# Feed-forward of the spatial block: seven products of halves for 20 of 22 column pairs, the down projection as its own phase

## What is computed

```python
def _conv_ffn(x, w_up, conv_f_w, conv_f_b, w_down):      # w_up 1024 x 5632, w_down 2816 x 1024
    h = _causal_depthwise_conv(x @ w_up, conv_f_w, conv_f_b)   # 3 taps along the 1024 rows
    gate, val = h[..., :D_FF_2], h[..., D_FF_2:]
    return (jax.nn.silu(gate) * val) @ w_down

x = _layernorm(DEEPNORM_ALPHA * x + ffn, ln2_g, ln2_b)
```

## Time and profile before

| | |
|---|---|
| median of 3 runs | 3779.22 us (3771.41 to 3779.77) |
| profiled execution: span, first to last instruction | 3767.9 us |
| its own time | not given apart from the runs; span and what lies around it, some 11 us at the median |
| PE busy | 3631.0 us, 96% |
| DVE, ACT, POOL busy | 57%, 34%, 48% |
| granted TensorE clock, mean | 0.987 |
| the stage `ffn`, first up matmul to the end of the span | from 3012.9 us |

### The profile page before, as it was taken

The page is one execution under the profiler, slowest core; times in us unless marked ns, Lnnn a source line. Parts: engine busy times, 40 slices in busy tenths (PEclk is TensorE's granted clock), DMA queues, the critical chain, the costliest instruction groups (busy, mean ns, idle before and its releaser), DMA issues.

```text
span 3767.9 us, 51125 instructions
## 1 busy us (share of the span) xinstructions
PE 3631.0 (96%) x17973; PEld 2944.0 (78%) x17973; DVE 2148.5 (57%) x3586; ACT 1263.4 (34%) x2051; POOL 1812.5 (48%) x1926
## 2 busy tenths in 40 slices
...
DMA packets 244572, 223.53 MB, mean 59 GB/s; under 512 B 12586, under 2 KB 194488, under 8 KB 244425
## 3 DMA queue, kind: packets, MB, share of 16 engines
...
## 4 chain that ended last, share of the span: by engine, by line
PE 59%; DVE 4%; ACT 2%; POOL 1%; issue 1%; DVEq 0%; ACTq 0%; POOLq 0%
PE PS L749 6%; PE PS L750 6%; PE PS L751 6%; PE PS L1219 3%; PE PS L1220 3%; PE PS L1221 3%; PE PS L776 3%; PE PS L778 3%; PE PS L777 3%; PE PS L871 2%; PE PS L869 2%; PE PS L870 2%; PE PS L883 2%; PE PS L885 2%; PE PS L884 2%; PE PS L1265 2%
## 5 line engine op out<-in xcount | busy, mean ns | idle before, releaser
L749 PE MATMUL PS<-UH,WH 128*128 128x512 f32 x1808 | 716.8, 396 | 22.4 <-ACT UU L2213 8.0
L3748 POOL TENSOR_SCALAR WH<-RAW 128x1024 fp32r<-128x1024 f32 x203 | 226.0, 1113 | 1033.0 <-issue 386.4
L3751 POOL TENSOR_TENSOR WL<-RAW,WH 128x256 fp32r<-128x256 f32 x809 | 704.1, 900 | 16.9
L751 PE MATMUL PS<-UH,WL 128*128 128x512 f32 x1808 | 708.1, 392 | 0.0
L750 PE MATMUL PS<-UL,WH 128*128 128x512 f32 x1808 | 707.9, 392 | 0.0
L749 PEld LDWEIGHTS PS<-UH,WH 128*128 128x128 f32 x1808 | 340.8, 188 | 103.1 <-issue 15.7
L751 PEld LDWEIGHTS PS<-UH,WL 128*128 128x128 f32 x1808 | 340.3, 188 | 73.8
L750 PEld LDWEIGHTS PS<-UL,WH 128*128 128x128 f32 x1808 | 341.0, 189 | 70.2 <-issue 0.2
L2423 DVE TENSOR_TENSOR X<-PS,X 128x512 f32<-128x512 f32 x320 | 215.3, 686 | 222.7 <-PE PS L935 213.5
L3376 DVE SCALAR_TENSOR_TENSOR FY<-FZ,PV,FY 128x512 f32<-128x512 f32 x88 | 82.9, 942 | 329.8 <-ACT FY L2343 328.9
L933 PE MATMUL PS<-WH,HH 128*128 128x512 f32 x640 | 253.9, 397 | 10.3 <-POOL WL L3751 5.6
...
## 6 DMA issues: line engine op xcount, KB each, us to landing
RAW<-in_mlp_w_dram SPq DMA_DIRECT2D x104, 512.0 KB, 4.2
...
RAW<-in_w_up_dram SPq DMA_DIRECT2D x44, 512.0 KB, 3.9
ADR<-in_ada_w_dram ACTq DMA_DIRECT2D x32, 512.0 KB, 3.8
WR<-in_od_w_in_dram SPq DMA_DIRECT2D x32, 512.0 KB, 4.2
W2R<-in_mlp_w_dram SPq DMA_DIRECT2D x24, 512.0 KB, 3.3
RAW<-in_w_down_dram SPq DMA_DIRECT2D x22, 512.0 KB, 3.2
RAW<-in_ev_w_in_dram SPq DMA_DIRECT2D x20, 512.0 KB, 3.8
```

Source lines behind the costliest of these rows:

```text
L749: pe.matmul(bank(b)[0:width], wh, xh, start=(k == 0), stop=False)
L751: mm = pe.matmul(bank(b)[0:width], wl, xh, start=False, stop=(k == NK - 1))
L3748: pool.tensor_scalar(WH[slot][:, 0:n], r[:, 0:n], 1.0, 1.0, ALU.mult, ALU.mult).then_inc(S("w_hi"), 1)
L3751: ins = pool.tensor_tensor(WL[slot][:, c], r[:, c], WH[slot][:, c].bitcast(F32), ALU.subtract)
```

## The change

The first two column pairs go as before (`up`). For each of the other 20, a round: x's transpose is cut in quarters (features 0 to 511 or 512 to 1023, tokens 0 to 511 or 512 to 1023), the pair's weights too (gate or val, upper or lower 512 features), and the four quarters of the result come from seven products, p1 to p7, in place of eight. US1, US2, US3 and UH's fourth quarter hold sums of quarters of x, made once by ACT, DVE and POOL. FT1, FT2, and the differences of p7 and p4 are made anew in each round by DVE (`t1_t2`, `t4`) and POOL (`t3`), and each of seven weight operands is split by ACT (`w_hi`) and POOL (`w_lo`) into one buffer per name. Products add up in banks b = r % 2, 6 and 7; ACT (`copy`) and DVE (`sum_`) take intermediate sums from a bank into GZ before the next product is added to it. ACT's `tap_2` writes the last tap into PSUM banks 2 to 5, DVE's `conv` adds the two others there, `silu` and `gated` make the result in FO, and SP writes it to DRAM (`ffn_gated`).

Then 11 blocks of the down projection: SP reads two row blocks back (FRAW, 1 MB), ACT and DVE split them (`f_hi`, `f_lo`), POOL splits w_down, PE does 16 items of 6 matmuls a block. The residual is scaled on DVE in rounds 2 to 9 (`residual`), from row vectors loaded by DMA; POOL's `resid(5, ...)` and PE's `t_rows(5, ...)` are gone. Semaphores are reused (`past` gives one with the count it starts from). The core of the diff, with its indentation shortened:

```diff
+FF_PLAIN = 2
+FF_ROUNDS = D_FF2 // P - FF_PLAIN
+FF_DOWN = D_FF2 // P // 2
+FF_SLOT = {"p1": (0, 0), "p2": (0, 1), "p6": (1, 0), "p5": (3, 0), "p7": (2, 0), "p3": (2, 1), "p4": (3, 1)}
+FF_ORDER = ("p1", "p2", "p6", "p5", "p7", "p3", "p4")
+FF_NTH = {name: i + 1 for i, name in enumerate(FF_ORDER)}
+FF_RES = 16
...
-    def down_half(h, order):
-        h_ready.take(2)
...
+    def product(r, name, b, start):
+        pe.wait_ge(*past("fp_lo", 7 * r + FF_NTH[name]))
+        xh, xl, k0, c = moving[name]
+        wh, wl = FPH[name], FPL[name]
+        for k in range(4):
+            if r == 0 and name in made:
+                pe.wait_ge(*past(made[name], k + 1))
+            w = slice(k * P, (k + 1) * P)
+            pe.matmul(bank(b), wh[:, w], xh[:, k0 + k, c], start=start and k == 0, stop=False, skip_group_check=True)
+            pe.matmul(bank(b), wh[:, w], xl[:, k0 + k, c], start=False, stop=False, skip_group_check=True)
+            mm = pe.matmul(bank(b), wl[:, w], xh[:, k0 + k, c], start=False, stop=(k == 3), skip_group_check=True)
+        mm.then_inc(S("fp_mm"), 1)
...
+    def round_(r):
+        b = r % 2
+        if r >= 2:
+            pe.wait_ge(*past("fp_c", 4 * (r - 1)))
+        product(r, "p1", b, True)
+        if r:
+            pe.wait_ge(*past("fp_d", 3 * (r - 1) + 1))
+        product(r, "p2", 6, True)
+        pe.wait_ge(*past("fp_c", 4 * r + 1))
+        product(r, "p6", b, False)
+        if r:
+            pe.wait_ge(*past("fp_d", 3 * r))
+        product(r, "p5", 7, True)
+        pe.wait_ge(*past("fp_c", 4 * r + 2))
+        product(r, "p7", b, False)
+        pe.wait_ge(*past("fp_c", 4 * r + 3))
+        product(r, "p3", 7, False)
+        pe.wait_ge(*past("fp_d", 3 * r + 2))
+        product(r, "p4", b, False)
...
+    def down(j, h, order):
+        s = j % 2
...
+            n = 16 * j + 8 * h + i
+            if n < 8:
+                name, count = FD_ENTRY[n]
+                pe.wait_ge(*past(name, count))
+            else:
+                pe.wait_ge(*past("fd_add", n - 7))
...
+            pe.wait_ge(*past("fd_w", 2 * j + 2 if h or order != BY_COLUMN[0] else 2 * j + mh + 1))
+            for k in range(2):
+                if i == 0:
+                    pe.wait_ge(*past("fd_lo", 4 * j + 2 * h + k + 1))
...
     up(0, 0, fresh)
-    t_rows(5, 0, 1)
     up(0, 1)
-    t_rows(5, 2, 3)
     t_u(5, 1, 0, 1)
     up(0, 2, None, {2: (2,), 5: (3,)})
     up(0, 3, None, {2: (4,), 5: (5,)})
     t_u(5, 1, 6, 7)
-    d_free.wait_at(ND)
-    with rounds(pe, ph["count"] - 1, (w_ready, 6), (a_free, 8), (d_free, 16), (h_ready, 4)) as it:
-        for m in range(4):
-            up(1, m, fresh if m == 0 else None)
-        down_half(0, BY_COLUMN[0])
-        for m in range(4):
-            up(0, m)
-        down_half(1, BY_COLUMN[1])
     for m in range(4):
-        up(1, m)
-    down_half(0, BY_BLOCK[0])
-    down_half(1, BY_BLOCK[1])
+        up(1, m, fresh if m == 0 else None)
+    a_free.wait_at(NA)
+    for r in range(FF_ROUNDS):
+        round_(r)
+    for j in range(FF_DOWN):
+        last = j == FF_DOWN - 1
+        for h in range(2):
+            down(j, h, (BY_BLOCK if last else BY_COLUMN)[h])
...
+    def w_hi(r, name):
+        if r == 0:
+            act.wait_ge(S("gemm_done"), item0 + 5 + FF_SLOT[name][0])
+        else:
+            act.wait_ge(*past("fp_mm", 7 * (r - 1) + FF_NTH[name]))
+        sem, count = {"p1": ("f_ra", 16 * (r + 1)), "p2": ("f_ra", 16 * (r + 1)), "p3": ("f_rb", 16 * (r + 1)),
+                      "p6": ("ft2", r + 1), "p5": ("ft1", r + 1), "p7": ("ft3", r + 1), "p4": ("ft4", r + 1)}[name]
+        act.wait_ge(*past(sem, count))
+        act.activation(FPH[name][:, :], src[name], ACT.Copy).then_inc(S("fp_hi"), 1)
+    def copy(r, nth, out, b):
+        act.wait_ge(*past("fp_mm", 7 * r + nth))
+        act.activation(out, bank(b), ACT.Copy).then_inc(S("fp_c"), 1)
...
+    def tap_2(r, m, z, b):
+        c = r + FF_PLAIN + 22 * m
+        act.activation(bank(b), z, ACT.Identity, bias=taps("conv_f_b_2", c), scale=taps("conv_f_w_2", c, 2))\
+            .then_inc(S("fp_y"), 1)
+    z = [GZ[:, m, 2 + h * HALF:2 + (h + 1) * HALF] for m in range(2) for h in range(2)]
+    def last_gate(r):
+        copy(r, 7, z[1], r % 2)
+        act.wait_ge(*past("fp_c", 4 * r + 4))
+        if r:
+            act.wait_ge(*past("fp_s", 2 * r))
+        tap_2(r, 0, z[1], 3)
+    def silu(r, h):
+        act.wait_ge(*past("fp_cv", 4 * r + (4 if h else 1)))
+        act.wait_ge(*past(f"f_sent{h}", 16 * (2 + r)))
+        act.activation(FO[h][:, :], bank(2 + h), ACT.Silu).then_inc(S("fp_s"), 1)
...
+    def f_hi(j):
+        act.wait_ge(*past("f_raw", 16 * (j + 1)))
+        if j == 1:
+            act.wait_ge(*past("fp_mm", 7 * _R + 6))
+        elif j >= 2:
+            act.wait_ge(*past("fd_mm", 16 * (j - 1)))
+        else:
+            act.wait_ge(*past("fp_mm", 7 * _R + 4))
+        for h in range(2):
+            for k in range(2):
+                act.activation(FSH[j % 2][:, k, half(h)], FRAW[:, k, half(h)], ACT.Copy).then_inc(S("fd_hi"), 1)
...
+    first_silu(0, 0)
+    first_silu(0, 1)
+    for k in range(4):
+        s_hi(3, k)
+    first_item(1, 0)
+    w_hi(0, "p1")
+    w_hi(0, "p2")
+    for k in range(4):
+        s_hi(2, k)
+    first_item(1, 1)
+    w_hi(0, "p6")
+    first_item(1, 2)
+    first_silu(1, 0)
+    first_item(1, 3)
+    w_hi(0, "p5")
+    for k in range(4):
+        s_hi(4, k)
+    first_silu(1, 1)
+    for k in range(4):
+        s_hi(1, k)
+    w_hi(0, "p7")
+    w_hi(0, "p3")
+    for r in range(FF_ROUNDS):
+        w_hi(r, "p4")
+        if r:
+            last_gate(r - 1)
+            act.wait_ge(*past("fp_cv", 4 * r))
+        else:
+            act.wait_ge(*past("f0_conv", 8))
+        copy(r, 1, z[0], r % 2)
+        if r:
+            silu(r - 1, 1)
+        nxt = r + 1 < FF_ROUNDS
+        if nxt:
+            w_hi(r + 1, "p1")
+        act.wait_ge(*past("fp_d", 3 * r + 1))
+        if r == 0:
+            act.wait_ge(*past("f0_f", 4))
+        else:
+            act.wait_ge(*past("fp_s", 2 * r - 1))
+        tap_2(r, 0, z[0], 2)
+        if nxt:
+            w_hi(r + 1, "p2")
+        silu(r, 0)
+        copy(r, 3, z[2], r % 2)
+        if nxt:
+            w_hi(r + 1, "p6")
+        copy(r, 4, z[3], 7)
+        if nxt:
+            w_hi(r + 1, "p5")
+            w_hi(r + 1, "p7")
+            w_hi(r + 1, "p3")
+        act.wait_ge(*past("fp_d", 3 * r + 3))
+        if r:
+            act.wait_ge(*past("fp_f", 2 * r))
+        tap_2(r, 1, z[2], 4)
+        tap_2(r, 1, z[3], 5)
+    f_hi(0)
+    last_gate(_R)
+    silu(_R, 1)
+    for j in range(1, FF_DOWN):
...
+    def t1_t2(r):
...
+    def t4(r):
+        if r == 0:
+            dve.wait_ge(S("gemm_done"), PH["ffn"]["I"] + 8)
+        else:
+            dve.wait_ge(*past("fp_mm", 7 * (r - 1) + 7))
+        dve.wait_ge(*past("ft2", r + 1))
+        dve.tensor_tensor(FPR["p4"][:, :], b21, FT2[:, :], ALU.subtract).then_inc(S("ft4"), 1)
...
+    def sum_(r, nth, m, h, b, c):
+        dve.wait_ge(*past("fp_mm", 7 * r + nth))
+        dve.wait_ge(*past("fp_c", 4 * r + c))
+        x = GZ[:, m, 2 + h * HALF:2 + (h + 1) * HALF]
+        dve.tensor_tensor(x, bank(b), x, ALU.add).then_inc(S("fp_d"), 1)
+    def conv(r, m, h, y_nth, cv_nth):
+        dve.wait_ge(*past("fp_y", 4 * r + y_nth))
+        c = r + FF_PLAIN + 22 * m
+        y = bank(2 + 2 * m + h)
+        x = lambda back: GZ[:, m, 2 + h * HALF - back:2 + (h + 1) * HALF - back]
+        fch.done(dve.scalar_tensor_tensor(out=y, in0=x(1), scalar=taps(c, 1), in1=y, op0=ALU.mult, op1=ALU.add))
+        dve.scalar_tensor_tensor(out=y, in0=x(2), scalar=taps(c, 0), in1=y, op0=ALU.mult, op1=ALU.add)\
+            .then_inc(S("fp_cv"), 1)
+    def gated(r, h):
+        dve.wait_ge(*past("fp_s", 2 * r + h + 1))
+        dve.wait_ge(*past("fp_cv", 4 * r + (3 if h else 2)))
+        dve.tensor_tensor(FO[h][:, :], bank(4 + h), FO[h][:, :], ALU.mult).then_inc(S("fp_f"), 1)
...
+    def residual(i):
+        q, step = i // 4, i % 4
+        x = X[:, 4 * (step % 2):4 * (step % 2) + 4, q * 256:(q + 1) * 256]
...
+                .then_inc(S("x5"), 1)
+            return
+        dve.wait_ge(*past("x5", i - 1))
+        dve.scalar_tensor_tensor(out=x, in0=b, scalar=ALPHA_2, in1=x, op0=ALU.mult, op1=ALU.add)\
+            .then_inc(S("x5"), 1)
...
+    for r in range(FF_ROUNDS):
+        if r:
+            t4(r)
+            conv(r - 1, 0, 1, 4, 4)
+        sum_(r, 2, 0, 0, 6, 1)
+        if r:
+            gated(r - 1, 1)
+        conv(r, 0, 0, 1, 1)
+        if r + 1 < FF_ROUNDS:
+            t1_t2(r + 1)
+        if 2 <= r < 2 + FF_RES // 2:
+            residual(2 * r - 4)
+            residual(2 * r - 3)
+        sum_(r, 5, 1, 1, r % 2, 3)
+        sum_(r, 6, 1, 0, 7, 2)
+        if r == _R:
+            f_lo(0, 0, 0)
+            f_lo(0, 0, 1)
+        conv(r, 1, 0, 2, 2)
+        conv(r, 1, 1, 3, 3)
+        gated(r, 0)
+    f_lo(0, 1, 0)
```

(72 more changed lines are left out.)

402 lines of the change are left out of this document (291 added, 111 removed), and 4 rows, old and new, of the table PAST.

## The result

The changed kernel takes 3782.67 us, the median of 19 runs (3778.98 to 3792.50). The kernel before, run beside it, takes 3773.47 us, the median of 19 (3768.28 to 3781.42). The ratio is 1.0026, 95% interval 1.0019 to 1.0033: slower by 9.2 us, which is inside the 0.3% called no change. 240 matmuls fewer, some 54 us, brought nothing.

The account below looks back on a forecast made before the run. It took TensorE's matmul count to bound the feed-forward stage. -54.4 - 7 + 4.9 + 42.2 + 25.5 + 2 + 1.7 = +14.9 us made the 3767.9 span 3783; 11.3 around it gave 3794 us, range 3762 to 3813.

Parts of the forecast that it names:

- slower by over 0.3%: Sign of the whole kernel's change: a time over 3790.5 us, chance 0.53.
- the drops: Granted clock falling to 1.2 GHz behind p6's wait: 15 of 19 rounds at 1.7 us, +25.5 us.
- round 0: First round of products: PE waits 3.2 us for copy(0, 1), and the clock drops, +4.9 us.
- 240 matmuls: Up phase: seven products leave 84 of a column pair's 96 matmuls, in 20 pairs, -54.4 us.
- entrance: Up to the first eight up items' end: transposes and gaps go, a new gap comes, net -7 us.
- stall, 19 rounds: PE stands 2.22 us ahead of p6 in each of 19 rounds, +42.2 us.
- residual, POOL: Rounds 2 to 9: residual's wide DVE operations beside POOL's weight pieces make w_hi p7 late, +2 us.
- exit and down: Down's first item waits for f_lo(0, 0, 1), +1.7 us; the down blocks after it cost nothing.
- The path: Each round, p3's end through DVE, ACT, DVE, ACT, DVE, ACT to p6: 10.38 us against 8.16 of PE work.
- the clock stays: Rival: same waits ahead of p6 but no clock drop, 3767 us, up to 3776 with a few; chance 0.18.
- POOL didn't set the round: Rival it denies: POOL's weight loop, some 24 us, sets each round, 3815 to 3825 us; chance 0.12.
- No stall: Rival: some handoff overlaps, the wait ahead of p6 is under 1 us, 3727 to 3742 us; chance 0.12.

Follow-up runs that it names:

- The two cuts: Against the changed kernel, w_hi(r, "p4") moved behind last_gate(r-1) on ScalarE: 3758.31 us; or t4(r+1) moved between conv(r, 1, 0) and conv(r, 1, 1) on VectorE: 3738.60 us.
- the two lengthenings: Against the changed kernel, t4(r) done three times in rounds 1 to 19: 3826.65 us; done twice: 3808.76 us.
- best3: The changed kernel with steps reordered on ScalarE, VectorE, GpSimd and in round 0, and residual spread one to a round over rounds 2 to 17: 3715.10 us, ratio 0.9839.

## Why the prediction was right and wrong

The number was 3794, the time 3782.7, inside the range of 3762 to 3813; the sign was right. But the likeliest case was "slower by over 0.3%", and the kernel is slower by 0.26%: the forecast of +14.9 on the profiled span, read as +20.5 over the median of 19 runs of before, was twice what came. The mechanism was right. What failed is two terms of the sum, the drops (15 forecast, 10 came) and round 0, and the base to which the sum was added. Term by term, in the profiled executions:

| term | forecast | measured | from |
|---|---|---|---|
| 240 matmuls | -54.4 | -54.4 | still 0.2267 us each; these terms and the 11.6 upstream make the 22.9 |
| entrance | -7 | -8.8 | end of the eighth up item 3072.81 to 3075.60, less 11.6 |
| round 0 | +4.9 | +14.4 | 41.05 us from there to p6 of round 1, less nine products and one stall |
| stall, 19 rounds | +42.2 | +42.0 | 19 x 2.21 |
| drops | +25.5 | +16.1 | 10 rounds longer by 1.6 |
| residual, POOL | +2 | +1.8 | four gaps of 2.25 to 2.45 us instead of 1.91 |
| exit and down | +1.7 | +1.7 | last product's end 3530.73 to the last pitch's end 3771.86, less 1056 x 0.2267 |
| tail | 0 | -1.5 | last matmul's pitch to the end: 20.5 us, then 18.9 |
| sum | +14.9 | +11.3 | |

- **The path was right,** in its sum, 10.23 for 10.27, and link by link within 0.06. It was walked in the code and priced from rows of other stages; the tap into PSUM, taken at 0.75 between 0.60 and 0.77, takes 0.78 in the median (0.76 to 0.79), just past the upper bound, and its handoff is as much shorter. The two cuts and the two lengthenings show that it is the cause.
- **The clock was mis-sized.** Four gaps of five in the earlier trace rows made a chance of 0.8; at 1.90 us it is 11 of 30. The five came from other stages, each with other work ahead of it, and five cases of such a share bound it poorly. The rows were misread as well: between the restart of 2709.64 and the fall of the clock stand two more gaps (0.71 and 0.98 us), the fall comes 3.0 us behind that restart and not within 2, and the shortest single gap with a drop is not 1.80 us but 1.63 (below). The price was right: 1.6 us for 1.7. The Trainium skill (TensorE: Matmul & The Clock Gate, HAM oscillation — how this bites in real kernels) tells of waits of some 3 to 5 us, each followed by the lower clock. The trace agrees at 3.35 us, 19 of 19; at 1.9 us, to which the prediction stretched it, it doesn't hold. The rival "the clock stays" was closer than its 0.18 said: at 1.5 us, 0.4 us shorter, no gap in this loop drops.
- **Round 0 failed.** I priced one wait, the one of 3.2 us, exactly (3.23), and stopped there. The next, 5.56 us ahead of p7, comes from SyncE's queue: raw_a(1) needs t4(0), done by 3084.3, but stands behind raw_b(1), which waits for POOL's split of p3 until 3088.7. The queue of SP was not walked, and a third gap, 1.33 us ahead of p1, was missed too. After such a start the clock falls again: 0.81 to 0.84 in 3080 to 3120.
- **The errors cancel.** +9.5 in round 0 against -9.4 in the drops. That the sum came near is luck.
- **The base was wrong.** I added 11.3 us for what lies around a span, from a median of three runs. Around the span lie 1.7 us, so the profiled run of before was one of some 3769.6, at the lower end of the 19, and the median of three (3779.2) was at the upper end. That is 5.7 of the 11.3 us by which 3794 is too high; the rest is +14.9 for +9.2. The profile gives +11.3, not +9.2, for the changed part; it is one execution, the longest of after, and where the 2.1 us between them lie, no run shows.
- **POOL didn't set the round,** as forecast: t4 kept its 0.68 in all 19 rounds, between 0.679 and 0.683. But the reason given, that the median shows a clash to be rare, is not why. GpSimd stood idle each time, since its next piece waits for the split that waits for t4:

```profile
3337.03 1.44 POOL L4163 TENSOR_TENSOR FPL_p<-FPR_p,FPH_p 128x256 fp32r<-128x256 f32 x2 [4.07 <-ACT FPH_p L2470]
```

The rule named beside it (the Trainium skill, SBUF — State Buffer, Who interferes with whom) showed in round 0, where t4 stands beside t3, 1.21 us, and in the later rounds as soon as t4 was moved beside a piece that POOL had begun, 1.16 to 1.31 us. It was right to hold the median for where t4 stood, and it would have been wrong for where the cure puts it.
- **The tail** was put at nothing, as the same instructions, and gave 1.5 us; it is 18.9 to 19.0 us in all twelve changed kernels. In before, one of DVE's last scalings runs beside POOL's last addition:

```profile
3752.43 3.20 POOL L3778 TENSOR_TENSOR X<-X,XB 128x1024 f32<-128x1024 f32 x1
...
3753.47 3.24 DVE L3419 SCALAR_TENSOR_TENSOR X<-X,RS,XB 128x1024 f32<-128x1024 f32 x1
```

In after POOL is through by then:

```profile
3774.85 2.35 POOL L4297 TENSOR_TENSOR X<-X,XB 128x1024 f32<-128x1024 f32 x1
...
3778.31 1.29 DVE L3742 SCALAR_TENSOR_TENSOR X<-X,RS,XB 128x1024 f32<-128x1024 f32 x1
```

- **"No stall"** was priced at 3727 to 3742 and called unlikely because every link is a wait in the code. So it is; but a few steps in another order remove it. Repaired in full, the change is worth 3715.1 - 3777.2 (before beside it) = -62 us by the medians; the matmuls and the entrance were put at -61.4. That the two meet is chance. In the profiles it is -55.6 (3715.0 - 3767.9, less 2.7 upstream): round 0 keeps 7.2 us (31.66 us from the eighth up item to p6 of round 1, less nine products), and the kernel before happened to be slow beside best3.
